# Hybrid attention and RG-LRU step, fp32 on one core: scores over two output banks in one product, row maxima one pair sooner, a clear moved to GpSimd

## What is computed

```
def attend_block(q_nope, q_pe, q_chunk, k_nope, k_pe, v, k_chunk):
    s = jnp.einsum("bqhd,bkhd->bhqk", q_nope, k_nope) + jnp.einsum("bqhr,bkr->bhqk", q_pe, k_pe)
    s = s.astype(jnp.float32) * SM_SCALE
    mask = k_chunk[None, :] <= q_chunk[:, None]
    s = jnp.where(mask[None, None], s, -1e30)
    w = jax.nn.softmax(s, axis=-1).astype(v.dtype)
    return jnp.einsum("bhqk,bkhd->bqhd", w, v)
```

## Time and profile before

| | us |
|---|---|
| median of 3 runs | 2670.52 (2668.87 to 2671.16) |
| the profiled execution | 2671.92 |
| its span, first to last instruction | 2668.9 |
| TensorE busy (matmul) | 2637.7 (99%) |
| VectorE busy | 1292.3 (48%) |
| ScalarE busy | 809.4 (30%) |
| GpSimd busy | 339.8 (13%) |
| score products, line 795, first and last start | 320.2 to 1801.3 |
| mean granted TensorE clock | 0.998 of full speed |

### The profile page before, as it was taken

How to read it: one execution, slowest core, us unless ns; L and a number is a source line. 1 busy time by engine, 2 the same in 40 slices (tenths; PEclk the granted TensorE clock), 3 DMA queues, 4 the chain that set the end, 5 groups by cost and what they waited for, 6 DMA issues and landing times.

```text
span 2668.9 us, 37085 instructions
## 1 busy us (share of the span) xinstructions
PE 2637.7 (99%) x15790; PEld 2547.7 (95%) x15790; DVE 1292.3 (48%) x1468; ACT 809.4 (30%) x1254; POOL 339.8 (13%) x215
## 2 busy tenths in 40 slices
PE   8999999999999999999999999999999999999998
PEld 8999877999999999999999998779999999999997
DVE  7898766563223222222368996765632232222323
ACT  4344355333112112022214434553320120220221
POOL 0123344120000000000201233431200000000001
PEclk9999999999999999999999999999999999999999
DMA  3112101211111111111221121012111111111112
GB/s 143 56 56 67 57 10 44 92 46 47 41 48 40 48 48 40 48 43 54 97 68 55 57 67 49 10 43 98 48 48 41 47 48 48 40 48 48 40 48 73
DMA packets 45450, 143.38 MB, mean 54 GB/s; under 512 B 8256, under 2 KB 12448, under 8 KB 45296
## 3 DMA queue, kind: packets, MB, share of 16 engines
q1 hardware_dynamic: 40384, 129.61, 14.6%
q0 software_dynamic: 4768, 11.45, 1.4%
q10 hardware_dynamic: 144, 0.04, 0.0%
HBM read 127.37 MB, written 11.36 MB: 52 GB/s over the span
## 4 chain that ended last, share of the span: by engine, by line
PE 97%; DVE 1%; issue 1%; ACT 0%; DMA 0%; SPq 0%; POOL 0%; DVEq 0%; ACTq 0%; POOLq 0%
PE ps L887 56%; PE ps L608 27%; PE ps L780 5%; PE ps L795 4%; PE ps L727 2%; PE ps L656 1%; PE ps L752 1%; PE ps L626 1%; DVE xall L1767 0%; PE ps L857 0%; DVE mxp L1612 0%; DMA qe<-mt 0%; DVE kol L1327 0%; DMA xall<-in_xT 0%; DVE srow L1635 0%
## 5 line engine op out<-in xcount | busy, mean ns | idle before, releaser
L1789 DVE TENSOR_TENSOR wlo<-raw,whi 128x1024 fp32r<-128x1024 f32 x126 | 154.4, 1226 | 921.2 <-ACT whi L1241 921.1
L1241 ACT ACTIVATE whi<-raw 128x1024 fp32r<-128x1024 f32 x126 | 133.6, 1061 | 979.1 <-PE ps L887 978.9
L887 PE MATMUL ps<-xmh,whi 128*128 128x358 f32 (+1 forms) x1536 | 334.4, 326 | 0.0
L887 PE MATMUL ps<-xml,whi 128*128 128x358 f32 (+1 forms) x1536 | 334.4, 326 | 0.0
L887 PE MATMUL ps<-xmh,wlo 128*128 128x358 f32 (+1 forms) x1536 | 334.2, 325 | 0.0
L887 PE MATMUL ps<-fl,whi 128*128 128x358 f32 (+1 forms) x1512 | 329.2, 326 | 0.0
L887 PE MATMUL ps<-fh,whi 128*128 128x358 f32 (+1 forms) x1512 | 329.2, 326 | 0.0
L887 PE MATMUL ps<-fh,wlo 128*128 128x358 f32 (+1 forms) x1512 | 328.8, 325 | 0.0
L887 PEld LDWEIGHTS ps<-xml,whi 128*128 128x128 f32 x1536 | 264.2, 189 | 0.0
L887 PEld LDWEIGHTS ps<-xmh,wlo 128*128 128x128 f32 x1536 | 264.1, 189 | 0.0
L887 PEld LDWEIGHTS ps<-xmh,whi 128*128 128x128 f32 x1536 | 263.7, 189 | 0.0
(11 more groups left out here) (292 smaller groups left out, 3926.1 us busy)
## 6 DMA issues: line engine op xcount, KB each, us to landing
raw<-in_wst SPq DMA_DIRECT2D x204, 512.0 KB, 3.5
xall<-in_xT SPq DMA_DIRECT2D x16, 537.0 KB, 6.4
x_scratch<-xall POOLq DMA_DIRECT2D x8, 537.0 KB, 3.8
xall<-x_scratch SPq DMA_DIRECT2D x8, 537.0 KB, 5.8
rc<-sum_scratch POOLq DMA_DIRECT2D x16, 268.0 KB, 4.1
out_yT<-xall SPq DMA_DIRECT2D x4, 768.0 KB, 4.3
ra<-qr SPq DMA_DIRECT2D x16, 134.2 KB, 2.4
out_ckv_out<-ckv POOLq DMA_DIRECT2D x4, 536.0 KB, 5.3
```

The lines of the kernel that those rows point to most:

```text
L887: mm = nc.tensor.matmul(to_slot(u, LIVE)(q), wt, (rh if c == "h" else rl)[kk](q), start=(kk == 0 and i == 0), stop=(kk == 7 and i == 2))
L1241: nc.scalar.activation(whi[b % 2][:, :], raw[b % 2][:, :], ACT.Copy).then_inc(S["w_hi"], 1)
L1789: V.tensor_tensor(wlo[b % 2][:, :], raw[b % 2][:, :], whi[b % 2][:, :].bitcast(F32), ALU.subtract).then_inc(S["w_lo"], 1)
```

## The change

- The two pairs of block 2 become one of 512 queries (208 to 720), the two of block 5 one of 448 (592 to 1,040): one score product in three passes, one set of exponentials. The PV product of such a pair is still made in two parts, one for each output bank (`parts_by_bank`). `NP` is 17. The tiles of the `pd` ring grow to 512 columns.
- The maxima groups stand in steps 1 to 10 instead of 2 to 12, groups 5 and 6 both in step 6. For head 1 (made in head 0) they stand in steps 3 to 10, two each in steps 5, 6 and 8. `MX_END` is 11, the transposition comes after step 12. `INVERT_AT` stays 10.
- The clear of row 32 for odd heads moves from VectorE's `load_q` to the head of GpSimd's `low_parts`. It waits for the same last scores and for the low parts of the head before, and TensorE's group 0 waits for it (`row_zero`).

```diff
@@ -138,44 +138,41 @@
-PAIRS = ([block_pair(t, 0) for t in (0, 1, 2)] + [block_pair(t, 1) for t in (3, 0, 4, 1, 5, 2)]
-         + [block_pair(6, 2), SAMPLE_PAIR] + [block_pair(t, 2) for t in (0, 7, 1, 2)] + [LAST_PAIR] + [block_pair(t, 2) for t in (3, 4, 5)])
+PAIRS = ([blocks(t, 0, 0) for t in (0, 1)] + [blocks(2, 0, 1)] + [blocks(t, 1, 1) for t in (3, 0, 4, 1)] + [blocks(5, 1, 2)]
+         + [blocks(6, 2, 2), SAMPLE_PAIR] + [blocks(t, 2, 2) for t in (0, 7, 1, 2)] + [LAST_PAIR] + [blocks(t, 2, 2) for t in (3, 4)])
-MX_AT = list(range(2, 13))
-MX_END = MX_AT[-1] + 1
...
+def parts_by_bank(pair):
+    _, _, q0, n, _ = pair
+    return [(b, max(q0, lo_), min(q0 + n, hi_)) for b, (lo_, hi_) in enumerate(Q_BANKS) if max(q0, lo_) < min(q0 + n, hi_)]
...
+def max_at(h):
+    return [3, 4, 5, 5, 6, 6, 7, 8, 8, 9, 10] if h == 1 else [1, 2, 3, 4, 5, 6, 6, 7, 8, 9, 10]
+MX_END = 11
...
+                        if h % 2 == 1 and h >= 3:
+                            w("row_zero", (h - 1) // 2)
...
-                        mm = nc.tensor.matmul(ps[0:65, bank, c0:c0 + n], v[:, v0:v0 + 65], p_tile(gk)[:, 0:n],
-                                              start=(k in FIRST), stop=(k in LAST))
+                        for g, qa, qb in parts_by_bank(PAIRS[k]):
+                            if k == BANK_FIRST[g] and hk >= 1:
+                                n_out = 3 * (hk - 1) + g + 1
+                                w("o_ev", n_out)
+                                w("s_ev", n_out)
+                            c0 = Q_BANKS[g][0]
+                            mm = nc.tensor.matmul(ps[0:65, O_BANKS[g], qa - c0:qb - c0], v[:, v0:v0 + 65], p_tile(gk)[:, qa - q0:qb - q0],
+                                                  start=(k == BANK_FIRST[g]), stop=(k == BANK_LAST[g]))
...
-                    if h % 2 == 1 and h >= 3:
-                        V.memset(qs[1][0][32:33, :].bitcast(F32), 0.0)
...
                 def low_parts(h):
+                    if h % 2 == 1 and h >= 3:
+                        w("s", (h - 1) * NP)
+                        w("q_lo", h)
+                        G.memset(qs[1][0][32:33, :].bitcast(F32), 0.0).then_inc(S["row_zero"], 1)
+                        w("row_zero", (h - 1) // 2)
```

More of the change, by code:

```diff
@@ L138, in first_seen, with blocks @@
     return 0 if t == 0 else P * t - 48
-def block_pair(t, bank):
-    lo_, hi_ = Q_BANKS[bank][0], min(Q_BANKS[bank][1], STREAM)
+def blocks(t, first, last):
+    lo_, hi_ = Q_BANKS[first][0], min(Q_BANKS[last][1], STREAM)
     q0 = max(lo_, first_seen(t))
@@ L154 @@
 OUT_LAG = LAG + 1
-MX_AT = list(range(2, 13))
-MX_END = MX_AT[-1] + 1
+Y_AT = [3, 6, 9, 14]
 INVERT_AT = 10
-Y_AT = [3, 6, 9, 14]
 DVE_CHAIN = 86
@@ L162 @@
 VW = 65 * NH
[L165 to L178, removed]
+def parts_by_bank(pair):
+    _, _, q0, n, _ = pair
+    return [(b, max(q0, lo_), min(q0 + n, hi_)) for b, (lo_, hi_) in enumerate(Q_BANKS) if max(q0, lo_) < min(q0 + n, hi_)]
+BANK_FIRST = [min(i for i, x in enumerate(PAIRS) if any(b == g for b, _, _ in parts_by_bank(x))) for g in range(3)]
+BANK_LAST = [max(i for i, x in enumerate(PAIRS) if any(b == g for b, _, _ in parts_by_bank(x))) for g in range(3)]
+assert all((g, Q_BANKS[g][0], min(Q_BANKS[g][1], STREAM)) in parts_by_bank(PAIRS[BANK_FIRST[g]]) for g in range(3))
+assert PAIRS.index(SAMPLE_PAIR) < PAIRS.index(LAST_PAIR) and max(x[3] for x in PAIRS) <= 512
 N_PART = 4
@@ L211 @@
 NMX = len(MAXES)
+def max_at(h):
+    return [3, 4, 5, 5, 6, 6, 7, 8, 8, 9, 10] if h == 1 else [1, 2, 3, 4, 5, 6, 6, 7, 8, 9, 10]
+MX_END = 11
+assert len(max_at(0)) == len(max_at(1)) == NMX and max(max_at(0) + max_at(1)) < MX_END
 P_RING = 3
@@ L319, in trunk @@
               [place("koh", "CK", 0, KW, F32R), place("kol", "CK", KB, KW, F32R)]]
[L320 to L323, removed]
+        P_END = 4 * TB + (2048 + 1536) * P_RING
+        pd = [place(f"pd{i}", "X", 4 * TB + 2048 * i, 512) for i in range(P_RING)]
+        pn = [place(f"pn{i}", "X", 4 * TB + 2048 * P_RING + 1536 * i, 384) for i in range(P_RING)]
+        pl = place("pl", "X", P_END, 64 + DEC)
+        ps_ = place("psmp", "X", P_END + 4 * (64 + DEC), DEC)
         def p_tile(g):
@@ L361, in trunk @@
         end_r = sb("end_r", [P, N_END])
-        mt = place("mt", "X", 4 * TB + 1536 * 2 * P_RING + 4 * (64 + 2 * DEC), 2 * P, F32R)
+        mt = place("mt", "X", P_END + 4 * (64 + 2 * DEC), 2 * P, F32R)
         mth, mtl = mt[:, 0:P], mt[:, P:2 * P]
@@ L771, in _ @@
                         kt, _, q0, n, _ = PAIRS[k]
-                        bank, c0 = o_place(q0)
                         w("p", gk + 1)
[L774 to L778, removed]
                         v0 = VW * kt + 65 * hk
-                        mm = nc.tensor.matmul(ps[0:65, bank, c0:c0 + n], v[:, v0:v0 + 65], p_tile(gk)[:, 0:n],
-                                              start=(k in FIRST), stop=(k in LAST))
+                        for g, qa, qb in parts_by_bank(PAIRS[k]):
[6 more added lines that the diff above has]
+                                                  start=(k == BANK_FIRST[g]), stop=(k == BANK_LAST[g]))
                         mm.then_inc(S["pv"], 1)
@@ L798, in _ @@
                     if h + 1 < NH:
-                        if i in MX_AT:
-                            max_step(h + 1, MX_AT.index(i))
+                        for s in range(NMX):
+                            if max_at(h + 1)[s] == i:
+                                max_step(h + 1, s)
                         if i == MX_END + 1:
@@ L1678, in _ @@
                         if h + 1 < NH:
-                            if i in MX_AT:
-                                reduce_max(h + 1, MX_AT.index(i))
+                            for s in range(NMX):
+                                if max_at(h + 1)[s] == i:
+                                    reduce_max(h + 1, s)
                             if h == 0 and i == 4:
```

4 lines of the change are left out of this document (1 added, 3 removed).

## The result

| | before | after |
|---|---|---|
| median, us | 2670.07 (5 runs) | 2683.42 (5 runs, 2679.92 to 2683.89) |
| ratio to before, 95% interval | | 1.0045 [1.0034, 1.0056] |
| the profiled execution, us | 2671.92 | 2679.92 |
| its span, us | 2668.9 | 2678.1 |
| heads 1, 3, 5 / 2, 4, 6, us | 19.53 / 20.56 | 20.15 / 21.80 |

The changed kernel is slower by 0.45%; 2685.6 us had been forecast, in a range of 2676 to 2691. A head's length is the distance between the PV products at which it and the next one start, in TensorE's timeline. The lengths in the table are of heads that wait for no shift row. Added up over both layers the attention loop grew by 11.5 us (5.6 and 5.9) between the two profiled executions; the rest of the program took 2.3 us less (0.5 ahead of the first loop, 0.9 between the two, 1.0 behind the second), which nothing here explains.

A forecast was written before the change was run, and what follows sets the result against it. The prediction took TensorE's queue, 97% of the chain, to bound the kernel. Its terms, −4.5 + 4.2 + 8.4 + 2.6 − 0.7 + 5.1 = +15.1 us, took the median of 2670.52 to 2685.6 us, range 2676 to 2691.

The forecast's parts named there:

- merged products: Score products in the attention loop: a merge saves 0.14 us, two per head and 16 heads, −4.5 us.
- head start without the clear: First maxima product of heads 1 to 6: TensorE waits 0.6 us for VectorE's casts, +4.2 us.
- exclusion of clear and casts: Start of heads 2, 4, 6: GpSimd's clear and VectorE's casts can't run together, 6 × 0.85, +5.1 us.
- head end, heads 1 to 6: Transposition of the row maxima waits for VectorE, 0.45 us in odd heads, 1.45 in even, +8.4 us.
- head 0: Maxima groups in head 0 wait behind the subtraction held by GpSimd: +2.6 us (1 to 4).
- shift rows: Next head's first scores wait less for DMAs, with 224 more PV queries after the transposition: −0.7 us.
- The case forecast as likeliest: Both VectorE chains come too late and clear and casts exclude each other: 2685.6 us, chance 0.52.
- Clear beside casts: Rival: at the start of even heads GpSimd's clear overlaps VectorE's casts, no 5.1 us: 2680.5 us, chance 0.28.
- The chains keep up: Rival: VectorE has casts, clear and maxima ready at head start and end, waits vanish: 2659.4 us, chance 0.08.
- Half the waits: Rival: hand-overs or small products cheaper, head 0 keeps its waits, loss shrinks: 2665 to 2677 us, chance 0.12.
- the widened products do nothing: Rival: a 128-query score product costs only its columns, so 4.5 us are missing: 2690 us, no chance given.

The follow-up runs named there:

- a4: The changed kernel with the clear of row 32 left out on both engines: 2677.01 us, 1.0022 of before.
- b1: The changed kernel measured once more, unedited: 2682.96 us, 1.0051 of before.
- a1: The changed kernel with the reciprocal at pair 8 instead of 10: 2676.63 us, 1.0029 of before.
- b2: The kernel before with nothing but the clear moved to GpSimd: 2667.62 us, 0.9994 of before.
- c1: The changed kernel with maxima steps rearranged from step 2 on, reciprocal at pair 7, output bank copies one pair sooner: 2657.96 us, 0.9956 of before.
- b3: The kernel before with nothing but the maxima one pair sooner, no pairs merged, clear on VectorE: 2680.26 us, 1.0042 of before.
- a3: The changed kernel with the clear of row 32 back on VectorE ahead of the casts: 2684.62 us, 1.0052 of before.

## Why the prediction was right

| term | forecast, us | measured, us | from |
|---|---|---|---|
| merged products | −4.5 | −5.7 | head 7, 16 × 0.36 |
| head start without the clear | +4.2 | +2.6 | 0.54, 0.50 and 0.43 in heads 1, 3, 5; 0.43 less 0.49 in even ones (a4) |
| exclusion of clear and casts | +5.1 | +5.3 | a4, 6 × 0.88 |
| head end, heads 1 to 6 | +8.4 | +6.8 | step 12, 0.40 and 1.22 less 0.49 |
| head 0 | +2.6 | +2.7 | 2.0 longer in all, 0.7 of merges |
| shift rows | −0.7 | −0.8 | heads 3 and 4 of the first layer and 5 of the second were 0.2 to 0.3 longer than their likes before |
| without a place | | +0.6 | what is left of 11.5 |
| granted clock in head 0 | none | up to +3 | b1 against after |

**What held.** The case forecast as likeliest is the one that came: both of VectorE's chains are too late, and clear and casts exclude each other. Waits of 0.54 and 1.3 us at the head's start stand against 0.6 and 1.4, 0.4 and 1.2 at its end against 0.45 and 1.45.

**Merges, mis-sized.** A merge gave 0.18 us instead of 0.14, the upper end of the bounds. The working took single steps of head 7; the whole head, 16.83 against 16.46, was not to be had before. Which of its steps holds the missing 0.04 is not shown.

**Head start, mis-sized.** The forecast read the casts' end, 1.95 us after the head's start, in head 1 and took it for all six heads. In head 1 VectorE is still at a weight split, which ends at 340.70 before, and the casts start 0.38 us after the head's start. In head 5, which starts at 421.10, they start 0.20 after it (before, VectorE's timeline) and are over after 1.77:

```profile
421.30 0.71 DVE L1585 CAST qe<-ra 32x1074 fp32r<-32x1074 f32 x1 [2.63 <-PE ps L795]
```

In after they start 0.31, 0.27 and 0.20 us after the start of heads 1, 3 and 5, and the waits are 0.54, 0.50 and 0.43 instead of 0.6. In even heads 0.43 takes the place of 0.49, where the forecast had 0.1 more.

**Head end, mis-sized.** The reciprocal was taken with its whole 0.98; a1 shows 0.83. The next instruction starts before the reciprocal's row is over (378.48 against 377.57 + 0.98), so a row's length is more than what it holds up. It is the same with two reductions and a copy: 356.46 against 355.67 + 0.86. A chain is the distance between starts, not a sum of lengths.

**The clear.** The one meeting of 0.06 us in the earlier trace rows bore the right answer: the cast ends 0.57 after the clear, as there (0.56). A better row was at hand: the 2.29 us of the earlier trace rows are a blocked row too (1.50 where GpSimd is not in the way), which is what the forecast meant by the subtraction that GpSimd holds; it ends 8.15 us after head 0's start before and 8.07 in after, hardly sooner, as forecast. The Trainium skill, page "SBUF — State Buffer", section "Who interferes with whom", calls the pair of ports that VectorE and GpSimd share an exclusive lock; 1.58 us instead of 0.71 in after, b2 and c1 agree with it, for a GpSimd operation that only writes one partition. On who blocks whom the rows don't bear the section out: the cast's row starts 0.02 to 0.03 us ahead of the clear's in all three, and it is the cast that waits; so small a distance may lie within what the profile can tell.

**Shift rows, right in size by another way.** After still has such a wait (0.3 us ahead of head 4's first scores), yet head 4 takes 21.78 us like heads 2 and 6: the time goes into the wait for the casts right behind it, not into the 224 queries of the forecast.

**Step missed.** Nothing in the sum foresaw that the stall in head 0 can bring TensorE down to its lower clock. The loop grew by 11.5 us at full clock where +15.1 was forecast; the medians differ by 13.35, and the step of 3 us between the executions has the size of the clock's cost in b1. So the forecast came closer to the median than its terms did, and that is luck: head start and head end were 3.2 too high together, the merges' gain 1.2 too small, and a cost of up to 3 was missing.

**Rivals.** Clear beside casts falls with the 1.58. The chains keep up falls with b3 (the maxima's place alone is +11 us) and is in a way what c1 makes true: 2657.96 against the 2659.4 worked out for it. Half the waits falls with the rows; the widened products do nothing falls with head 7.

## What to carry to other kernels

Pulling work forward in the queue of the engine that bounds the kernel only pays up to where its inputs are ready: read, for the place it is to stand, the distance from the event that releases the producer's chain to the chain's end, and compare it with the steps left in front. Work that is removed or moved away in front of a wait is lost in the wait, so put the waits right first; here the same merges gave nothing in the odd heads of the changed kernel and 0.36 us a head once four settings of the order were changed. A side task such as a reciprocal or a copy of sums belongs outside the last stretch of the chain that the bound engine waits for. Before moving a small operation to an engine that seems free, look for a row, such as the earlier trace rows, that is longer than its likes while that engine is at work.

## What the runs showed of the hardware

- A VectorE cast of 32 x 1074 from SBUF to SBUF that meets a GpSimd clear is recorded with 1.58 us instead of 0.71, and no idle time says so: a wait inside an instruction shows in its length alone. A row longer than its likes is the sign. A VectorE subtraction of 64 x 1296 that meets a GpSimd subtraction takes 2.2 to 3.1 us instead of 1.50 and ends 1.36 to 1.37 us behind it, however long they overlap (0.8 to 1.8 us).
- TensorE's granted clock was 0.50 over 331 to 335 us of b1, behind a wait of 1.84 us, and 1.00 over the same stretch of after, behind one of 1.67: the same kernel, 3 us apart.
- Released by the same product, VectorE's clear of one partition is recorded 0.24 us later than its cast of 32 (0.44 and 0.20 us after the head's start, a3 and after).
- A reciprocal of 0.98 us held up the next instruction by 0.91, and by 0.83 the one that TensorE waited for.
